# Whole weight blocks, a later load of constants, and half of a norm's squares taken early

## The reference

```
for l in (0, 1):
    h = rmsnorm(x, norm_mix[l]) * (1 + scale) + shift      # shift, scale, gate from silu(cond) @ ada_w[l]
    if l == 0: o = concat(windowed attention, multi-scale pooling) @ a_w_out
    else:      o = fft2_real(h @ f_w_in, over tokens and features) @ f_w_out
    x = x + gate * o
    h = rmsnorm(x, norm_ffn[l]) * (1 + scale) + shift
    # top-1 group of 4, in it top-2 of 4 experts; 16 experts in all
    x = x + gate * sum over chosen experts e of comb[e] * ((silu(h @ w1[e]) * (h @ w3[e])) @ w2[e])
```

## Time and profile before

| what | value |
|---|---|
| median of three runs | 793.98 us |
| profiled execution, its time | 790.84 us |
| its span in the trace | 789.0 us |
| PE busy | 765.7 us (97%) |
| DVE busy | 343.9 us (44%) |
| ACT busy | 176.7 us (22%) |
| DMA, mean over the span | 351 GB/s |
| granted PE clock | 0.999 |

### The profile page before, as it was taken

The page is one execution under the profiler, slowest core; times in us unless marked ns, Lnnn a source line. Parts: engine busy times, 40 slices in busy tenths (PEclk is TensorE's granted clock), DMA queues, the critical chain, the costliest instruction groups (busy, mean ns, idle before and its releaser), DMA issues.

```text
span 789.0 us, 10240 instructions
## 1 busy us (share of the span) xinstructions
PE 765.7 (97%) x3991; PEld 377.7 (48%) x3991; DVE 343.9 (44%) x783; ACT 176.7 (22%) x433; POOL 2.2 (0%) x9
## 2 busy tenths in 40 slices
PE   7999999999999999999999899999999999999997
PEld 3364545545553454444334657645454444345434
DVE  2226188214841742643345512325732643445326
ACT  4111566204521111101111601105321101101111
POOL 0000000000000000000000000000000000000000
PEclk9999999999999999999999999999999999999999
DMA  8979999932899999999999982024599999999995
GB/s 344 423 235 430 426 429 427 419 151 84 343 372 404 422 422 419 422 420 422 420 417 422 430 361 108 1 108 173 197 391 423 422 420 422 419 422 421 421 417 221
DMA packets 41779, 277.13 MB, mean 351 GB/s; under 512 B 8781, under 2 KB 9825, under 8 KB 13825
## 3 DMA queue, kind: packets, MB, share of 16 engines
q1 hardware_dynamic: 41233, 275.03, 85.2%
q10 hardware_dynamic: 432, 1.28, 0.4%
q0 software_dynamic: 64, 0.13, 0.0%
HBM read 274.72 MB, written 1.70 MB: 350 GB/s over the span
## 4 chain that ended last, share of the span: by engine, by line
PE 83%; DMA 8%; DVE 4%; ACT 2%; issue 1%; DVEq 1%; SPq 1%; ACTq 0%
PE bank L2014 26%; PE bank L2039 13%; PE bank L1884 10%; DMA ring<-in_moe_w 6%; PE bank L1993 5%; PE bank L2445 5%; PE bank L2045 5%; PE bank L2308 4%; PE bank L1823 4%; PE bank L2269 2%; DMA ring<-in_ada_w 2%; PE bank L2360 1%; PE bank L2381 1%; PE bank L2025 1%; PE bank L2020 1%
## 5 line engine op out<-in xcount | busy, mean ns | idle before, releaser
L2014 PE MATMUL bank<-ring,Z 128*64 128x512 f32 x1024 | 226.8, 594 | 1.7 <-DMA ring<-in_moe_w 1.7
L2014 PEld LDWEIGHTS bank<-ring,Z 128*64 128x64 f32 x1024 | 72.7, 137 | 138.8 <-issue 136.6
L2039 PE MATMUL bank<-ring,Z 128*64 128x512 f32 (+1 forms) x544 | 113.9, 570 | 0.0
L1884 PE MATMUL bank<-ring,T 128*128 128x512 f32 x192 | 83.1, 592 | 0.0
L2039 PEld LDWEIGHTS bank<-ring,Z 128*64 128x64 f32 x544 | 37.5, 137 | 68.3 <-issue 66.2
L1496 DVE TENSOR_TENSOR Z<-Z,bank 128x512 f32<-128x512 f32 x16 | 11.0, 688 | 121.9 <-PE bank L2014 121.9
L1884 PEld LDWEIGHTS bank<-ring,T 128*128 128x128 f32 x192 | 36.2, 190 | 44.0 <-issue 44.0
L2045 PE MATMUL bank<-ys,Cs 128*128 128x512 f32 (+1 forms) x204 | 52.3, 391 | 1.1 <-DVE ys L1513 1.1
L1526 DVE TENSOR_TENSOR x<-x,bank 128x512 f32<-128x512 f32 x84 | 52.1, 682 | 0.2
L1160 ACT ACTIVATE ys<-wg 128x512 fp32r<-128x512 f32 (+1 forms) x34 | 20.6, 606 | 133.9 <-DVE wg L1508 133.9
L1823 PE MATMUL bank<-ring,cond 128*32 128x512 f32 x384 | 45.8, 598 | 3.9 <-DMA ring<-in_ada_w 3.6
(11 more groups left out here) (243 smaller groups left out, 751.8 us busy)
## 6 DMA issues: line engine op xcount, KB each, us to landing
ring<-in_moe_w SPq DMA_DIRECT2D x184, 1024.0 KB, 15.5
ring<-in_ada_w SPq DMA_DIRECT2D x23, 2048.0 KB, 16.0
ring<-in_moe_w SPq DMA_DIRECT2D x16, 512.0 KB, 21.1
ring<-in_a_w_out SPq DMA_DIRECT2D x2, 2048.0 KB, 14.6
ring<-in_f_w_in SPq DMA_DIRECT2D x2, 2048.0 KB, 27.3
ring<-in_f_w_out SPq DMA_DIRECT2D x2, 2048.0 KB, 30.9
ring<-in_ada_w SPq DMA_DIRECT2D x2, 1024.0 KB, 8.9
ring<-in_a_w_in SPq DMA_DIRECT2D x4, 512.0 KB, 19.2
```

Source lines behind the costliest of these rows:

```text
L1884: last = pe.matmul(b[:, :], T[:, k, i * P:(i + 1) * P], w[:, k, :], start=(k == 0), stop=(k == KT - 1))
L2014: last = pe.matmul(out[BLK * u:BLK * (u + 1), :], xT[:, b, k, s0 + BLK * u:s0 + BLK * (u + 1)], w[:, k, :], start=(k == 0), stop=(k == KT ...
L2039: last = pe.matmul(out, aT[:, k, BLK * u:BLK * (u + 1)], down_columns(w2, k, a, e), start=(k == 0), stop=(k == FC - 1), skip_group_check=True)
```

## The change

Four things:

1. Expert items 0 to 6 and 18 to 41 are loaded as whole blocks of 2 MB in the order of their numbers (`whole_block`), with one semaphore each; PE waits for the whole block before the product starts (`in_halves` says which items still have halves). Items 7 to 17 and the last pair stay in halves; 17 is now alone in its turn.
2. The load of the rest of the constants goes behind `z_part(1)` instead of ahead of `ada_w` item 1.
3. DVE's wait for these constants and its three copies go behind its bank copies of the first projections.
4. At the end of layer 0, ACT squares and sums the first 512 columns of each tile as soon as they are added back: tiles 0 and 1 before it makes the high part of the last column range, tile 2 after it. Behind the Sqrt that loads the table come a drain and one small Identity that turns the three sums into the bias (sum/D + eps); the norm then squares only the last 512 columns and takes Sqrt(sum/D + bias).

```diff
--- before.py
+++ after.py
@@ -535,6 +535,7 @@
         ckT_in = sb("ckT_in", [P, KVW])
         cv = sb("cv", [P, KVW])
         stat = sb("stat", [P, 2, NT])
+        first_squares = sb("first_squares", [P, 2, NT])
 
 
         z = Z[:, 0:NT * ZW].rearrange("p (t n) -> p t n", t=NT)
@@ -783,9 +784,16 @@
                 if 0 <= n - n_exp[l] < 3 * NE:
                     return l, (n - n_exp[l]) // 6, (n - n_exp[l]) % 6
 
+        def in_halves(n):
+
+            if not expert_item(n):
+                return False
+            l, p, m = expert_item(n)
+            return NS <= 6 * p + m < 3 * 6 or p == NPAIR - 1
+
         def late_count(n):
 
-            return 16 * sum(expert_item(i) is not None for i in range(n % NS, n + 1, NS))
+            return 16 * sum(in_halves(i) for i in range(n % NS, n + 1, NS))
 
         def last_use(n, half=1):
 
@@ -873,10 +881,11 @@
                 sp.dma_start(x[:, t, :], x_sample[0, (t - 1) * P:t * P, :]).then_inc(x_in[t], 16)
                 if t == 1:
                     z_part(0)
-            sp.dma_start(cst[:, early:], const[:, early:]).then_inc(const_in, 16)
             for j in range(1, 4):
                 weights(j + 1, before0[j + 1])
                 z_part(j)
+                if j == 1:
+                    sp.dma_start(cst[:, early:], const[:, early:]).then_inc(const_in, 16)
             for n, src in enumerate(before0):
                 if n > 4:
                     weights(n, src)
@@ -904,14 +913,22 @@
                             u, w = items[j % 6]
                             expert_words(2 * (j // 6) + u, j, w, half, SLOT // 2 * half, SLOT // 2 * (half + 1))
 
+                def whole_block(j):
+                    u, w = items[j % 6]
+                    weights(n0 + j, w[l, 2 * (j // 6) + u])
+
+
 
 
                 for j in range(NS):
-                    blocks_in_turn(j)
+                    whole_block(j)
 
                 blocks_in_turn(*range(NS, NS + 4))
-                for j in range(NS + 4, 6 * (NPAIR - 1), 2):
-                    blocks_in_turn(*range(j, min(j + 2, 6 * (NPAIR - 1))))
+                for j in range(NS + 4, 3 * 6 - 1, 2):
+                    blocks_in_turn(j, j + 1)
+                blocks_in_turn(3 * 6 - 1)
+                for j in range(3 * 6, 6 * (NPAIR - 1)):
+                    whole_block(j)
                 sp.wait_ge(plan_ready, l + 1)
                 blocks = sp.value_load(plan_i[0:1, NOV:NOV + 1], min_val=0, max_val=NOV)
                 with sp.If(blocks > 0):
@@ -1154,10 +1171,18 @@
                     act.wait_ge(s["mid_full"], p + 1)
                     act.activation(aT, psA[:, :].rearrange("p (k s) -> p k s", k=FC), ACT.Copy).then_inc(s["act_cols"], 1)
 
-                def down_high(s, p, w, parts=((0, HALF), (HALF, D))):
-                    for n, (a, e) in enumerate(parts):
-                        act.wait_ge(s["gated_out"], 2 * p + n + 1)
-                        act.activation(ys[0:w, 0, a:e], wg[0:w, a:e], ACT.Copy).then_inc(s["down_high"], 1)
+                def high_part_of(s, p, w, n, a, e):
+                    act.wait_ge(s["gated_out"], 2 * p + n + 1)
+                    act.activation(ys[0:w, 0, a:e], wg[0:w, a:e], ACT.Copy).then_inc(s["down_high"], 1)
+
+                def down_high(s, p, w):
+                    for hh in range(2):
+                        high_part_of(s, p, w, hh, HALF * hh, HALF * (hh + 1))
+
+                def squares_of_first_half(i):
+
+                    act.wait_ge(s["back_out"], (NPAIR - 1) * 2 * NT + i + 1)
+                    act.activation(h[:, i, 0:HALF], x[:, i, 0:HALF], ACT.Square, accum_out=first_squares[:, 0, i:i + 1])
 
                 def pair(s, p, b):
                     silu(s, p)
@@ -1183,14 +1208,26 @@
                             hidden_cols(o, j)
                             down_high(o, j, BLK)
                 pair(s, NPAIR - 1, 1)
-                down_high(s, NPAIR - 1, 2 * BLK, END_PARTS)
+                for n, (a, e) in enumerate(END_PARTS):
+                    if l == 0 and n == len(END_PARTS) - 1:
+                        squares_of_first_half(0)
+                        squares_of_first_half(1)
+                    high_part_of(s, NPAIR - 1, 2 * BLK, n, a, e)
+                if l == 0:
+                    squares_of_first_half(2)
 
             for l in range(L):
                 if l == 1:
 
                     act.activation(stat[:, 1, 0:1], con("eps"), ACT.Sqrt)
+                    act.drain()
+                    act.activation(first_squares[:, 1, :], first_squares[:, 0, :], ACT.Identity, scale=1.0 / D, bias=con("eps"))
                     for i in range(NT):
-                        rms(2, i)
+                        act.wait_ge(x_ready, NT + i + 1)
+                        act.activation(h[:, i, HALF:], x[:, i, HALF:], ACT.Square, accum_out=stat[:, 0, i:i + 1])
+                        act.drain()
+                        act.activation(stat[:, 1, i:i + 1], stat[:, 0, i:i + 1], ACT.Sqrt, scale=1.0 / D,
+                                       bias=first_squares[:, 1, i:i + 1]).then_inc(rms_ready, 1)
                     affine(2, 0)
                     affine(2, 1)
                     ada_product(21)
@@ -1628,10 +1665,6 @@
                 ada_read(j)
                 first_affine(j, 0)
                 first_affine(j, 2)
-            dve.wait_ge(const_in, 16)
-            dve.tensor_copy(before_bf, con("before"))
-            dve.tensor_copy(ones_bf, con("ones"))
-            dve.tensor_copy(spread.rearrange("p k n -> p (k n)"), cst[:, CONST["spread0"][0]:CONST["spread0"][0] + 2 * P])
             for cc in range(len(W_IN_COLS)):
                 for i in range(NT):
                     if turn[("z", cc, i)][2] == "dve":
@@ -1639,6 +1672,10 @@
                         w, a = W_IN_COLS[cc], sum(W_IN_COLS[:cc])
                         emptied_inc(dve.tensor_copy(z[:, i, a:a + w], b[:, 0:w]))
 
+            dve.wait_ge(const_in, 16)
+            dve.tensor_copy(before_bf, con("before"))
+            dve.tensor_copy(ones_bf, con("ones"))
+            dve.tensor_copy(spread.rearrange("p k n -> p (k n)"), cst[:, CONST["spread0"][0]:CONST["spread0"][0] + 2 * P])
             dve.wait_ge(params_in, loads[params_in])
             dve.tensor_copy(sink[:, :].rearrange("p (c k) -> p k c", k=NKV), sink_in[:, :].rearrange("p (k c) -> p k c", k=NKV))
             dve.wait_ge(qk_squares, 1)
@@ -2060,7 +2097,8 @@
                     def arrive(k, half):
                         for n in (n0 + 6 * p + k, n0 + 6 * p + k + 1):
                             if half:
-                                pe.wait_ge(arrived_late[n % NS], late_count(n))
+                                if in_halves(n):
+                                    pe.wait_ge(arrived_late[n % NS], late_count(n))
                             else:
                                 pe.wait_ge(arrived[n % NS], 16 * (n // NS + 1))
```

## The result

| | before | after |
|---|---|---|
| median of 7 runs each | 791.32 us (790.19 to 794.58) | 787.23 us (786.71 to 788.99) |
| ratio, 95% interval | | 0.9947 [0.9929, 0.9965] |
| profiled execution, its span | 790.84, 789.0 | 787.51, 785.6 |

The change takes 4.1 us off the median and 3.3 to 3.4 us off the traced execution. The seven runs of before contain the three that the forecast knew; their median of 793.98 was high, and larger groups of its runs (8 to 35), taken later beside the experiments, gave 790.7 to 791.0.

A forecast was written before the change was run, and what follows sets the result against it. TensorE, busy 765.7 of 789.0 us, was taken as the bound, with about 3.3 us of waits touched. Terms -0.8 + 0 - 1.25 - 0.2 + 0 = -2.25 us gave 791.7 us from the 793.98 median; range 787.5 to 795.5.

The forecast's parts named there:

- The level: Whole kernel: 793.98 us, the median of three runs, taken as the time before the change.
- A: Experts: slower weights in some executions make the gain -4.2 us, up to -5.2; 789.5, best 787.5; chance 0.27.
- Whole blocks: Expert pairs 6 and 7: pace and order cut weight waits, -1.25 us in layer 0, -0.2 in layer 1.
- The pace: Expert items 18 to 41: whole blocks load at 427 GB/s against 421 for halves, 0.07 us less a block.
- the 0.2 us wait: Layer 0, pair 6's second w3 product: a wait of 0.2 us stays in place of 0.58.
- Squares: Layer change: what is won at the row's end is lost at its head, 0 us; ends -0.3 and +1.0.
- the 0.13 us delay of the high part: Layer change: the last high part starts 0.13 us late, behind an early Square and its sum's read.
- Constants later: Start: the 0.96 us wait before adaLN item 1 goes, 0.1 to 0.2 comes before item 2; -0.8 us.
- VectorE's copies: Start: three casts, under 0.9 us, move ahead of a reduce where VectorE stands idle 1.79 us; 0 us.
- B: Experts: the 427 GB/s belongs to the adaLN weights, nothing comes of the blocks; -0.4 us, 793.6; chance 0.14.
- C: Items 18 to 41: whole blocks come slower than halves, +2.6 us in sum, 796.6; chance 0.07.
- D: Layer change comes late, +1.0 to +1.3 us on the forecast, 792.8; chance 0.07.

The follow-up runs named there:

- e1: Whole blocks alone put into the kernel before; 788.19 us, ratio 0.9974.
- e3: Early squares alone put into the kernel before; 790.02 us, ratio 0.9992.
- e2: Constants' load and VectorE's copies moved later, alone, in the kernel before; 789.58 us, ratio 0.9985.
- e4: Kernel before with the second halves of expert items 18 to 35 not loaded in either layer; 788.08 us, ratio 0.9971.
- e12: Changed kernel without tile 2's early square, and with items 11 to 17 whole too; 788.09 us, ratio 0.9959.
- e6: Changed kernel with each whole expert block loaded as two 1 MB transfers of 64 partitions; 1028.45 us, ratio 1.301.
- e9: Changed kernel with items 18 to 41 loaded two at a time, as 2 MB transfers with 8 KB rows; 794.58 us, ratio 1.0040.

## Why the prediction was too small

The time missed by 4.5 us: 791.7 forecast, 787.2 measured. Of this 2.7 us is the level (793.98 taken for a kernel that has 791.3 over seven runs), and 1.8 us the change (-2.25 forecast, -4.1 measured). The steps that failed are the level, the price of the whole blocks, taken from the waits of one execution, and the squares, put at nothing.

- **The level.** From three runs I took 793.98 as the kernel's time and placed the range by it; 71 further ones put it near 791. The forecast's own -2.25 from there would be 788.8, and 787.2 would lie within a range of the same width. A median of three with 4.4 us between its members was no base for bounds to the half us, and the same scatter was the sign of A.
- **Whole blocks, -1.25 and -0.2: measured -1.8 and -0.07 in the two traces, -2.6 in all over the nine traces. This is the mis-sized term.** The pace held (427 to 428), and so did the direction of every step. But the term was bounded by the waits of one execution, 1.45 and 0.20 us. The queue's lateness is not a property of the kernel but of the execution, 7.6 to 10.9 us in the traces, and halves lose up to 2.4 us a layer by it. Besides, the recorded wait isn't the whole price of a broken product (about 0.4 us more for the two in layer 0). Item 39 landed 178.1 us after the first product before and 172.1 after, 6.0 us sooner where 4.0 was forecast: 0.9 of the rest is the smaller lateness (9.2, 8.3), and about 1.2 what before's queue lost on top of its pace in that layer. So the 0.2 us wait that I kept didn't come. That e1's item 39 lands at 386.0, where the forecast moved by e1's own start has 386.2, is luck: its queue was 1.1 us further behind (10.3) and didn't lose the 1.2.
- **Squares, 0: measured -0.46** in the two traces and the same in e3's, though e3's runs can't tell it from zero. The head of the row came late as worked out (0.8 for 0.9) and VectorE took ScalarE's place, yet the projection came 0.2 us sooner: the 0.13 us delay of the high part didn't occur, because the read of the sum ends only 0.1 us behind its Square. The other 0.25 stands at the router, a place that the forecast didn't look at, and has no explanation.
- **Constants later, -0.8: right.** The 0.96 wait went whole and the new wait before item 2 is 0.18 (0.1 to 0.2 forecast): -0.79 from the same point on. The other 0.28 of the -1.07 arises at item 0, where executions of one kernel differ by more than that. e2 alone: -1.1 by the medians.
- **VectorE's copies, 0: right.** The reduce behind their new place starts 12.86 us after the second part of the projection in both traces (62.59 - 49.73 and 61.52 - 48.66).
- **The rest, from -3.4 to -4.1.** It is not a term of the change: 0.9947 [0.9929, 0.9965] includes the 0.9957 of the two traces, and against the later groups of before the difference is 3.4 to 3.8 us. Averages over the traces give -0.8 - 2.6 - 0.5 = -3.9.
- **Rival A**, given 0.27, had the reason right that the forecast lacked: executions differ in how late the experts' weights come, and whole blocks take that away. The table of the traces and the spreads of e1 and e4 show it. Its size was too large: 4.2 to 5.2 us on the experts and the start, where the traces give 3.4.
- Rivals B and C fell with the windows (427), D with the timeline. One slip in a bound: at 430 GB/s a block takes 4.88 us, 0.10 less than at 421 and not 0.09, so that end is 2.5 us by item 41, A's best 5.8, and the range built from it would begin at 786.9. The time would lie in it, by luck.

## What to carry to other kernels

A wait of 1 or 2 us for a queue that runs at its limit is a sample from a distribution: look at how far behind the queue was, over several executions, before pricing what a faster queue gives. Long rows pay as soon as the queue is deep; small pieces pay where slots are released late and the queue is short, and a boundary wrong by a few items (e12, 1.8 us) costs most of what the long rows give. When work is moved ahead of a table load, count what the load then holds up: two tiles' squares fit into waiting time, the third stood in the way (0.6 us). And a trace can be typical in its total and not in its parts: before a part is priced, read it in several executions.

## What the hardware showed that I hadn't expected

- Loads that alternate between the lower and the upper 64 partitions ran at 220 GB/s with all 16 engines busy (share 1.01), half of the 428 of the same rows over 128 partitions. By the Trainium skill ("SBUF — State Buffer", section "Door 1: The DMA port swizzle"), partitions 0 to 63 reach only 8 of the memory's 16 ports, and 64 to 127 the other 8; e6 agrees with it.
- Over all 128 partitions, 8 KB rows go at 420 to 421 GB/s with 1 MB or 2 MB a transfer (417 in one of e9's windows), and 16 KB rows at 427 to 428 with 2 MB. The Trainium skill's "DMA: Bandwidth & Descriptors", section "Bandwidth", gives 341 GB/s for a transfer of 1 MB issued from GpSimd; in a SyncE queue that is never empty no such loss shows.
- TensorE's granted clock fell to 0.77 on average where it stood idle for 42% of a stretch (e6), and is 1.00 in all other windows shown.
- How far a weight queue is behind at one and the same place, with the same loads issued at the same times, differs between executions by up to 3.3 us (7.6 to 10.9).
